# Product-key expert layer: table writes, first gate loads and VectorE's item order at the seam between gate tables and dense part

## What is computed

```python
q = (xn @ w_query).reshape(T, 8, 2, 128)
s = einsum('thpc,hpkc->thpk', q, sub_keys)          # 8 heads, 2 halves, 128 keys
s1, i1 = top_k(s[:, :, 0], 16); s2, i2 = top_k(s[:, :, 1], 16)
cand_s = s1[..., :, None] + s2[..., None, :]        # 256 pairs, best 16 of them
top_s, pos = top_k(cand_s.reshape(T, 8, 256), 16)
idx = take_along_axis(i1 * 128 + i2, pos); gates = softmax(top_s)
act = gelu(einsum('tkd,td->tk', expert_u[idx], xn)) # 128 experts for each token
out = einsum('tk,tkd->td', gates * act, expert_v[idx])
```

## Time and profile before

| | us |
|---|---|
| median of 3 runs | 2651.85 |
| the profiled execution, its own time | 2652.4 |
| its span | 2650.7 |
| PE busy | 2509.4 |
| DVE busy | 1953.4 |
| POOL busy | 1436.2 |
| ACT busy | 430.6 |

### The profile page before, as it was taken

How to read it: one execution, slowest core, us unless ns; L and a number is a source line. 1 busy time by engine, 2 the same in 40 slices (tenths; PEclk the granted TensorE clock), 3 DMA queues, 4 the chain that set the end, 5 groups by cost and what they waited for, 6 DMA issues and landing times.

```text
span 2650.7 us, 24105 instructions
## 1 busy us (share of the span) xinstructions
PE 2509.4 (95%) x7657; PEld 1380.6 (52%) x7657; DVE 1953.4 (74%) x4210; ACT 430.6 (16%) x790; POOL 1436.2 (54%) x1169
## 2 busy tenths in 40 slices
PE   8999999998878899999999999999999999999993
PEld 7687785876756344444444444444444444444441
DVE  3207678668669788686988867769787687877878
ACT  1212223313678100100010100000000000001010
POOL 0000220678762256676756757657576675666665
PEclk9999999998999899999999999999999999999996
DMA  8543763666589979999999999999999999999998
GB/s 320 188 165 143 296 260 127 191 199 180 134 234 257 363 271 391 348 361 415 381 388 402 383 419 353 389 401 387 419 389 397 384 349 420 391 404 395 371 372 306
DMA packets 285918, 857.88 MB, mean 324 GB/s; under 512 B 41952, under 2 KB 97248, under 8 KB 271200
## 3 DMA queue, kind: packets, MB, share of 16 engines
q0 software_dynamic: 167184, 541.73, 54.8%
q1 hardware_dynamic: 108336, 289.45, 28.9%
q10 hardware_dynamic: 10272, 25.17, 2.4%
HBM read 807.94 MB, written 48.30 MB: 323 GB/s over the span
## 4 chain that ended last, share of the span: by engine, by line
PE 69%; POOL 11%; DVE 7%; DMA 5%; issue 4%; ACT 1%; DVEq 1%; another core or an unknown queue 0%; ACTq 0%; POOLq 0%
PE pairs L779 29%; PE pairs L733 27%; POOL gate_tables L597 8%; PE pairs L646 7%; POOL ring L626 4%; PE pairs L691 3%; DMA ring<-in_expert_u,idx 3%; PE pairs L665 2%; DVE arena L1339 1%; DMA gate_tables<-gate,place 1%; DVE junk L1122 1%; ACT pick_all L812 1%; DMA arena<-gate_tables 1%; PE pairs L658 0%; DVE work L1002 0%
## 5 line engine op out<-in xcount | busy, mean ns | idle before, releaser
L626 POOL DMA_INDIRECT ring<-in_expert_u,idx x512 | 650.8, 1271 | 575.7 <-DVE dots L1122 307.7
L779 PE MATMUL pairs<-arena 128*128 128x512 f32 x2048 | 885.5, 594 | 13.7 <-DVE arena L1185 11.2
L733 PE MATMUL pairs<-arena 128*128 128x512 f32 x2048 | 882.8, 592 | 3.8 <-ACT arena L929 3.8
L1122 DVE CUSTOM_DVE_ANT_0 junk<-ring,xf 128x1024 bf16<-128x1024 f32 x512 | 612.1, 1223 | 182.6 <-DMA ring<-in_expert_u,idx 177.2
L626 POOL DMA_INDIRECT ring<-in_expert_v,idx x512 | 567.0, 1107 | 326.4 <-DVE arena L1133 149.0
L779 PEld LDWEIGHTS pairs<-arena 128*128 128x128 f32 x2048 | 389.8, 191 | 506.9 <-issue 502.3
L733 PEld LDWEIGHTS pairs<-arena 128*128 128x128 f32 x2048 | 388.5, 190 | 490.5 <-issue 490.5
L1133 DVE SCALAR_TENSOR_TENSOR arena<-ring,arena 128x1024 f32<-128x1024 f32 x381 | 473.4, 1283 | 97.4 <-DMA ring<-in_expert_v,idx 92.3
L646 PE MATMUL pairs<-arena 128*128 128x256 f32 (+1 forms) x1792 | 403.3, 388 | 10.9 <-ACT arena L882 9.7
L646 PEld LDWEIGHTS pairs<-arena 128*128 128x128 f32 x1792 | 342.9, 192 | 69.2 <-ACT arena L882 10.3
L597 POOL DMA_INDIRECT gate_tables<-gate,place x128 | 211.7, 1654 | 166.0 <-DVE gate L1141 102.3
(11 more groups left out here) (160 smaller groups left out, 1088.4 us busy)
## 6 DMA issues: line engine op xcount, KB each, us to landing
arena<-in_w_all SPq DMA_DIRECT2D x80, 1024.0 KB
arena<-in_uT SPq DMA_DIRECT2D x128, 512.0 KB
arena<-in_expert_v SPq DMA_DIRECT2D x128, 512.0 KB
arena<-gate_tables SPq DMA_DIRECT2D x32, 1024.0 KB
gate_tables<-arena SPq DMA_DIRECT2D x12, 2048.0 KB
gate_tables<-junk ACTq DMA_DIRECT2D x4, 2048.0 KB, 13.8
ring<-in_expert_u,idx POOLq DMA_INDIRECT x512
ring<-in_expert_v,idx POOLq DMA_INDIRECT x512
```

The costliest lines, as they stand in the source:

```text
L626: nc.gpsimd.indirect_dma_start(out=ring[:, r % RING, :], out_offset=None, in_=expert_u if table == "u" else expert_v, in_offset=bass.Indir ...
L733: last = nc.tensor.matmul(score_bank[x], uslot[:, x % USLOTS, k * P:(k + 1) * P], xfT[:, k, :], start=(k == 0), stop=(k == KD - 1))
L779: last = nc.tensor.matmul(o_bank[n % 4], gated[:, x % GSLOTS, t * P:(t + 1) * P], vrows[:, j, half * 512:(half + 1) * 512], start=(j == 0) ...
L1122: nc.vector.tensor_tensor_reduce(out=junk[:, r % 2, :], in0=row, in1=xf[:, t % 2, :], scale=1.0, scalar=0.0, op0=ALU.mult, op1=ALU.add, ac ...
```

## The change

Six things. The last chunk is written by two DMAs, its first two groups (of 32) by themselves, with a semaphore of their own. SP then waits only for these (and for the other stage) before it asks for gates 0; it waits for the rest of the chunk between V7 and gates 1. The residual's load is issued ahead of U10 to U13. FIRST_FILL is 26 in place of 54. Eight gates (VJ), not ten, stand in a row at that place, and the share counts from eight. And a `digits` unit is held back until the next three items to be laid are all sums; a `pick` that comes before that releases it.

```diff
@@ constants
-FIRST_FILL = 54.0
+FIRST_FILL = 26.0
@@ VectorE's order
-        order, done = [], 0
+        order, done, held = [], 0, []
...
             if i == first_fill:
-                order += items[:EARLY]
-                done = EARLY
-            order.append(unit)
+                order += items[:VJ]
+                done = VJ
+            if unit[0] == "pick" and held:
+                order.append(held.pop())
+            if unit[0] == "digits":
+                held.append(unit)
+            else:
+                order.append(unit)
+            if held and done + 2 < len(items) and all(k == "sum" for k, _, _ in items[done:done + 3]):
+                order.append(held.pop())
...
-            until = min(len(items), EARLY + int((len(items) - EARLY) * share * DENSE_SPEED))
+            until = min(len(items), VJ + int((len(items) - VJ) * share * DENSE_SPEED))
@@ SP, the write of chunk c
+                if c < TABLE_CHUNKS - 1:
+                    sp.dma_start(to, of).then_inc(table_kept[c % STAGES], 16)
+                else:
+                    sp.dma_start(to[:, 0:2], of[:, 0:2]).then_inc(first_kept, 16)
+                    sp.dma_start(to[:, 2:], of[:, 2:]).then_inc(table_kept[c % STAGES], 16)
@@ SP, behind V0 to V2
-            for c in range(STAGES):
+            for c in range(last_stage):
+                stage_kept(c)
+            sp.wait_ge(first_kept, 16)
             sp.wait_ge(scattered, 16 * HK)
             load_gates(0)
             for j in range(3, VJ):
                 load_v(0, j)
+            stage_kept(last_stage)
             load_gates(1)
+            sp.dma_start(sums, ...).then_inc(d_h2_in, 16)
             while next_u < EARLY + USLOTS:
                 load_u(next_u)
                 next_u += 1
-            sp.dma_start(sums, ...).then_inc(d_h2_in, 16)
```

More of the change, by code:

```diff
@@ L289, in program @@
         table_kept = [sem(f"table_kept{i}") for i in range(STAGES)]
+        first_kept = sem("first_kept")
         xfT_in = sem("xfT_in")
@@ L537, in _ @@
                 sp.wait_ge(table_out, (c + 1) * (CHUNK // 4))
-                sp.dma_start(g_d[:, :, FIRST_CHUNK + c, :].rearrange("g p n -> p g n"),
-                             tables[:, c % STAGES].rearrange("p (g j) t -> p g (j t)", j=GJ)).then_inc(table_kept[c % STAGES], 16)
+                to, of = g_d[:, :, FIRST_CHUNK + c, :].rearrange("g p n -> p g n"), tables[:, c % STAGES].rearrange("p (g j) t -> p g (j t)", j=GJ)
+                if c < TABLE_CHUNKS - 1:
[3 more added lines that the diff above has]
+                    sp.dma_start(to[:, 2:], of[:, 2:]).then_inc(table_kept[c % STAGES], 16)
             sp.wait_ge(table_full, 2 * BATCHES)
@@ L543, in _, with stage_kept @@
                 load_v(0, j)
-            for c in range(STAGES):
+            def stage_kept(c):
                 sp.wait_ge(table_kept[c], 16 * ((TABLE_CHUNKS - 1 - c) // STAGES + 1))
+            last_stage = (TABLE_CHUNKS - 1) % STAGES
+            assert last_stage == STAGES - 1
+            for c in range(last_stage):
+                stage_kept(c)
+            sp.wait_ge(first_kept, 16)
             sp.wait_ge(scattered, 16 * HK)
@@ L549, in _ @@
                 load_v(0, j)
+            stage_kept(last_stage)
             load_gates(1)
+            sp.dma_start(sums, h2_d[0:DENSE_TILES, :, :].rearrange("t p d -> p t d")).then_inc(d_h2_in, 16)
             while next_u < EARLY + USLOTS:
@@ L553, in _ @@
                 next_u += 1
-            sp.dma_start(sums, h2_d[0:DENSE_TILES, :, :].rearrange("t p d -> p t d")).then_inc(d_h2_in, 16)
             pending = []
```

## The result

In 20 runs of each kernel on several chips the kernel before has a median of 2653.32 us and the changed kernel one of 2658.64 us. The ratio of runs on the same chip is 1.002, with a 95% interval of 1.0012 to 1.0029: 5.3 us slower, between 3.2 and 7.7. That is the side of the forecast (2661, 9 us slower), and inside its range. The profiled execution took 2658.53 us with a span of 2656.8.

What follows compares the result with a forecast made beforehand. TensorE was taken as the bound, VectorE's list up to S2.0 right behind; piece 2.4 +6.5 us and half clock +3.1, less some 0.6, gave +9 us: 2661 us, range 2647 to 2669.

Steps and rivals of the forecast that it cites:

- The gates asked for first, eight early: Start of the seam: gate loads land 890.8 and 900, VectorE 5 us later, piece 0.7 ends 2.6 us earlier.
- The places: Before pick 6: ScalarE's places move beside sums, TensorE's 3.77 us go, but S2.0 slips to 1169.2, piece 2.4 +6.5 us.
- 1146.0 + 5 + 0.6 - 4 = 1147.6: Time row 183 is done: G24's earlier end, plus VectorE's lag, plus G25, less what comes back of the DMA hole.
- + 5: VectorE's lag behind the early gates, 5 us, carried through whole to row 183.
- - 4: Before row 183: only the hole in the DMA share, 0.2 x 20 = 4 us, comes back.
- 12.1 us of digits and stall: VectorE before row 183: digits 4.1 us and the 7.95 us wait before G18 go, mostly becoming waits for rows.
- rival A: Gathered rows catch up, G25 done by 1134.7, S2.0 costs TensorE nothing: -6.6 us, 2645 us; chance 0.12.
- forecast C: The forecast itself: S2.0 late, TensorE waits before piece 2.4, half clock behind; 2657 to 2665 us, chance 0.44.
- rival B: Nearly no change: G25 done between 1136 and 1143.5, or the clock stays up; 2647 to 2657 us, chance 0.29.
- bound of 1157: Before piece 2.4: S2.0 done before 1157 would show the forecast wrong and the rows caught up.
- D: All late, towards the upper bound, and piece 2.0 also waits for G23; 2665 to 2672 us, chance 0.15.

Runs made afterwards that it cites:

- e5: The kernel before with only the row of eight gates from FIRST_FILL = 26, SP as before: ratio 0.9984.
- e4: The kernel before with only SP's part (last chunk in two writes, gates asked for behind the first, residual ahead of U10): ratio 1.0004.
- e1: The changed kernel without the holding of the digits: ratio 0.9996 to the kernel before.
- e2: The kernel before with only the holding of the digits: ratio 1.0034.
- e7: The changed kernel with pick 6 moved behind S2.2, digits still held: ratio 0.9966 to the kernel before.
- e6: The changed kernel with digits 6 right behind S1.3 and the gates placed where their tables land: ratio 0.9954 to the kernel before.
- e3: The changed kernel with digits 6 right behind S1.3 instead of held: ratio 0.9980 to the kernel before.
- e9: The changed kernel, digits still held, with the gates placed where their tables land: ratio 0.9987 to the kernel before.
- e10: The changed kernel, digits held, with the gates where their tables land and pick 6 behind S2.2: ratio 0.9939 to the kernel before.
- e3b: The kernel before with only digits 6 moved, to behind S1.2: ratio 0.9986.

## Why the prediction was right, and where not

**The gates asked for first, eight early.** Forecast for VectorE: waits of 12.5 us at G0 and 6.7 at G4, none at G8. Measured: 12.43, 6.39, none. Piece 0.0 was put at 894.4 and came at 894.5 (895.76 less 1.25); piece 0.7 was to end at 963.1 and ended at 962.8. The wait for S0.0 was put at 5 us and is 4.84. The 6 us of waits for S0.1 to S0.3 are only 2.6 of waits; 2.3 more went at the half clock behind the 4.84, which the forecast had not reckoned there. That piece 0.7 ends where it was put is owed to VectorE, which sets the pace there, whatever TensorE's clock.

SP asked for the load of G0 to G3 later than was thought. The forecast has the written groups there near 868 to 870, but SP stood in the issue of three V loads until 877.2:

```profile
869.14 8.03 SPq L532 DMA_DIRECT2D arena<-in_expert_v  x3
877.28 0.50 SPq L537 DMA_DIRECT2D arena<-gate_tables  x1
```

That is 4.8 us earlier than in the earlier trace rows, with the 1.25 taken off, and VectorE got the load 14.8 us later, behind the V loads; in e5, where SP asks as before, it got it 0.4 us after that. The landing at 890.8 came out (892.10 - 1.25 = 890.85), since the bytes ahead were the same. Order within a ring is what the Trainium skill states (DMA: Bandwidth & Descriptors, Queues, rings and completion order); the trace agrees, and e4 and e5 find no gain from SP's part that can be told from none.

**The places.** The gap at tile 22 went, and the pick waits 8.60 us, where 8 to 9 was said. S2.0 decides when piece 2.4 starts, half clock follows, then no gap to the end. The mechanism stands, and e1, e2 and e7 show it by taking it away, adding it alone and stepping round it.

**The term of the sum that was mis-sized** is "1146.0 + 5 + 0.6 - 4 = 1147.6", the time at which row 183 is done: it was 1145.09 - 1.25 = 1143.8. Two parts of it were off. Its part "+ 5", the lag of VectorE carried through, did not hold: at row 158 the kernel was 2.6 us behind before, 2.0 for the same work, since G18 now stands ahead of that row. Its part "- 4" was too small: from there to row 183 the lag fell by 4.2, to 1.6 us ahead of before, with one gate more done (0.6), so that 4.8 came back for the same work. The rest of the 12.1 us of digits and stall turned into waits for rows, as forecast, but less of it: summed over these rows of the timelines they are 14.2 us instead of 7.6. Together, 1146.0 + 2.0 + 0.6 - 4.8 = 1143.8.

Where did the lag go? Row 90 shows it still whole, 969.62 - 1.25 against this row of the kernel before, 5.2 us:

```profile
963.17 1.22 DVE L1122 CUSTOM_DVE_ANT_0 junk<-ring,xf 128x1024 bf16<-128x1024 f32 x1
...
1073.22 1.23 DVE L1122 CUSTOM_DVE_ANT_0 junk<-ring,xf 128x1024 bf16<-128x1024 f32 x1 [0.73 <-DMA ring<-in_expert_u,idx]
```

The second line is row 150 before; after has it at 1074.97, so the lag is 0.5 us. It was 6.4 at row 114, 4.5 at row 126, 2.2 at row 132. Between rows 114 and 150, which lie between the bursts of V loads, VectorE waits 9.9 us for rows in the kernel before and 3.8 in the kernel after: a VectorE that comes later waits less. That is rival A's mechanism, though most of it came before the stretch of 1060 to 1080 us that A named (the lag was 1.6 at row 128 and still at row 145). Nor does the lag fall evenly: it was 9.3 us at row 95 and 1.8 at row 106, each of the two kernels waiting for rows at other places. I had left this to the rival, where it should have stood in the sum. In the next burst of V loads the lag grew again, to the 2.6 of row 158. With 3.8 us less at row 183, S2.0 was done at 1165.0 and not 1169.2. The gap was 9.79 us, not 13.1, and the half clock took 30.03 - 27.6 = 2.4, not 3.1. The sum by measured terms: 1165.1 - 1162.7 + 2.4 = 4.8, the difference of the seams, beside 5.3 (3.2 to 7.7) by the ratio.

**The rivals.** The case came out at the border of the forecast C and rival B. B's condition was G25 done between 1136 and 1143.5, and it was done at 1144.03 - 1.25 = 1142.8, row 183 1.1 us after it; and 5.3 us is the very line that the prediction drew between B and C. So the mechanism and the side were right, but that the time falls to C and not to B is less than its interval of 3.2 to 7.7 us can tell, and partly luck. Of the 4.8 us of the seams 2.4 are S2.0 and 2.4 the half clock behind it, which B, where "S2.0 costs what the seam gained", left out. A had its mechanism right and its end wrong: the lag was made up, but S2.0 was 8 us too late for its bound of 1157 all the same. Nothing of D was seen.

## What to carry to other kernels

A unit that must wait for another engine belongs where enough work lies between its cause and its wait, and where nothing urgent is queued behind it. Ask both of each candidate place: the hold answered "is the wait beside something harmless?" for the cause, and put the wait itself right ahead of the one sum that had 2.6 us to spare. And asking for data earlier in a queue that serves in order, or using it earlier in a list than it lands, buys little; laying other work in until it lands bought 7 to 9 us (e6 over e3, e9 over the changed kernel, e10 over e7), and 12 to 16 together with a cure for the pick.

## What the runs showed of the hardware

What an idle stretch of TensorE costs at the clock does not follow its length. The gap of 3.77 us before tile 22 in the kernel before left the granted clock at 1.00 in the earlier trace rows, and its 64 records took 27.70 us. A shorter one of 2.81 us stands at the same place in e4, whose VectorE list is that of before; the 64 records behind it took 1.8 us more than 27.63, and the granted clock was 0.73 for 6.3 us. In e1 and e5 the gap stands one tile later; 3.39 and 3.62 us cost 3.1 and 2.8 more. PE and the stretch behind the gap in e4:

```profile
1100.83 29.40 PE L748 MATMUL pairs<-arena 128*128 128x512 f32 x64 [2.81 <-ACT arena L944]
1100.80:1107.10 6.30, 6.27 (x11) 2.79 (x12) 6.30 (x11) 1.32 (x3) 3.67 (x3) 0.73 0.48 165
```

The stretch behind the gap in e1:

```profile
1104.00:1112.00 8.00, 7.70 (x11) 3.32 (x12) 7.81 (x13) 1.60 (x4) 5.09 (x3) 0.60 0.74 281
```

Likewise 2.02 us in e3 cost 1.7 more, and 2.00 in e3b and 2.39 in the changed kernel nothing; 9.79 us in the changed kernel cost 2.4, and 5.75 in e9 2.8. Whoever prices a gap of 2 to 4 us should carry both ends, 0 and 3 us; I could not tell from any row which of them comes.
